# A decoder trunk with three attention mixers: low parts of query stacks and weight chunks made on VectorE in the stage of compressed blocks

## What is computed

```python
kcmp = compress(kc, pe_k, wk1, wk2)
vcmp = compress(vc, pe_v, wv1, wv2)
cend = jnp.arange(ncmp) * CMP_STRIDE + CMP_LEN - 1
dist_c = t[:, None] - cend[None, :]
valid_c = dist_c >= 0
sc = jnp.einsum('bsgrd,bcgd->bgrsc', q, kcmp).astype(jnp.float32) * scale
sc = sc - slopes[:, :, None, None] * dist_c.astype(jnp.float32)
p_cmp = jax.nn.softmax(jnp.where(valid_c, sc, NEG), axis=-1) * valid_c
o_cmp = jnp.einsum('bgrsc,bcgd->bsgrd', p_cmp.astype(vcmp.dtype), vcmp)
imp = jnp.einsum('bgrsc,cj->bsgj', p_cmp, overlap_matrix(ncmp, n_slc))
...
score = jnp.where(causal[:, None, :], jnp.where(forced[:, None, :], FORCE, imp), NEG)
_, idx = lax.top_k(score, topn)
...
return gates[..., 0:1] * o_cmp + gates[..., 1:2] * o_slc + gates[..., 2:3] * o_win
```

## Time and profile before

| | |
|---|---|
| median of three executions | 933.0 us |
| the profiled execution's own time | 934.59 us |
| its span | 932.5 us |
| mean granted TensorE clock | 0.946 |
| TensorE (PE) busy | 835.9 us, 90% |
| VectorE (DVE) busy | 568.5 us, 61% |
| ScalarE (ACT) busy | 432.5 us, 46% |
| GpSimd (POOL) busy | 171.4 us, 18% |

### The profile page before, as it was taken

How to read it: one execution, slowest core, us unless ns; L and a number is a source line. 1 busy time by engine, 2 the same in 40 slices (tenths; PEclk the granted TensorE clock), 3 DMA queues, 4 the chain that set the end, 5 groups by cost and what they waited for, 6 DMA issues and landing times. The chain is left out here.

```text
span 932.5 us, 19153 instructions
## 1 busy us (share of the span) xinstructions
PE 835.9 (90%) x7748; PEld 706.9 (76%) x7748; DVE 568.5 (61%) x1305; ACT 432.5 (46%) x969; POOL 171.4 (18%) x123
## 2 busy tenths in 40 slices
PE   3999999969898888689889993989999999979997
PEld 3899887757686767578778872878887988868885
DVE  4841111136989888567639982878787877843332
ACT  5621111034565555357433322677777787732221
POOL 0233000030312231021045310141010323031220
PEclk9999999989899999699979995999999999979999
DMA  7220226052314122061254316000001111032431
GB/s 267 101 114 1 73 97 169 12 148 82 97 64 123 36 91 69 27 174 44 68 134 107 91 46 174 2 2 2 3 2 47 47 48 47 3 113 94 133 135 45
DMA packets 31942, 73.04 MB, mean 78 GB/s; under 512 B 5104, under 2 KB 13680, under 8 KB 30832
## 3 DMA queue, kind: packets, MB, share of 16 engines
q1 hardware_dynamic: 31856, 71.83, 24.8%
HBM read 55.57 MB, written 16.25 MB: 77 GB/s over the span
## 5 line engine op out<-in xcount | busy, mean ns | idle before, releaser
L1677 DVE SCALAR_TENSOR_TENSOR n_probsT_low<-n_turned,n_probsT_high 128x512 f16<-128x512 f32 (+3 forms) x192 | 94.4, 520 | 32.1 <-ACT n_probsT_high L1612 29.8
L1602 ACT ACTIVATE n_probs<-n_probs,n_negated_max 128x640 f32<-128x640 f32 (+7 forms) x128 | 94.0, 734 | 26.4 <-DVE n_negated_max L1668 25.7
L1612 ACT ACTIVATE n_probsT_high<-n_turned 128x512 f16<-128x512 f32 (+3 forms) x192 | 81.1, 457 | 37.7 <-PE n_turned L657 35.4
L657 PE MATMUL n_turned<-identity,n_probs 128*128 128x128 f32 x528 | 82.2, 280 | 16.1 <-ACT n_probs L1602 15.7
L1770 PE MATMUL n_scores<-w_and_keys_high,stacks 128*128 128x256 f32 (+2 forms) x192 | 78.5, 409 | 3.9 <-DVE n_negated_max L1668 2.5
L657 PEld LDWEIGHTS n_turned<-identity,n_probs 128*128 128x128 f32 x528 | 61.0, 143 | 23.7 <-ACT n_probs L1602 17.9
L153 POOL TENSOR_TENSOR w_and_keys_low<-w_raw,w_and_keys_high 128x1024 fp32r<-128x1024 f32 x15 | 38.2, 2546 | 154.1 <-ACT w_and_keys_high L146 153.9
L1771 PE MATMUL n_scores<-w_and_keys_low,stacks 128*128 128x256 f32 (+2 forms) x192 | 63.2, 336 | 0.0
L1668 DVE CUSTOM_DVE_ANT_0 n_probs<-n_scores,n_bias_full 128x1024 f32<-128x1024 f32 (+3 forms) x64 | 48.3, 754 | 20.0 <-PE n_scores L1774 19.9
L580 PE MATMUL nat<-stacks,xT_high 128*128 128x256 f32 (+1 forms) x192 | 56.0, 292 | 2.8 <-DVE stacks L452 2.6
L785 ACT ACTIVATE a_probsT_high<-a_turned 128x512 f16<-128x512 f32 (+3 forms) x48 | 21.8, 489 | 74.0 <-PE a_turned L657 74.0
(11 more groups left out here) (266 smaller groups left out, 2540.8 us busy)
## 6 DMA issues: line engine op xcount, KB each, us to landing
w_raw<-in_w_feat SPq DMA_DIRECT2D x23, 512.0 KB, 3.7
features<-staged SPq DMA_DIRECT2D x30, 256.0 KB, 2.0
a_raw<-features SPq DMA_DIRECT2D x36, 128.0 KB, 2.7
s_raw<-features SPq DMA_DIRECT2D x18, 256.0 KB, 4.3
branches_b_c<-in_x SPq DMA_DIRECT2D x8, 512.0 KB, 5.1
silu_gates<-staged SPq DMA_DIRECT2D x16, 256.0 KB, 2.0
gatesT<-silu_gates SPq DMA_DIRECT2D x8, 512.0 KB, 5.4
keys_and_w_out_raw<-in_w_out SPq DMA_DIRECT2D x4, 1024.0 KB, 4.8
```

What stands on the lines that cost most here:

```text
L657: mm = nc.tensor.transpose(dst[:, j, :], src[:, c:c + P], ident[:, :])
L1602: nc.scalar.activation(pr[:, n % PS, 0:w], pr[:, n % PS, 0:w], ACT.Exp, scale=-1.0, bias=nmax[:, hb % 4, qt:qt + 1], accum_out=sums[:, hb ...
L1612: nc.scalar.activation(pth[:, g % GS, 0:k, :], tp[g % TS][:, 0:k, :], ACT.Copy, scale=PSCALE).then_inc(t_high, 1)
L1677: nc.vector.scalar_tensor_tensor(out=ptl[:, g % GS, 0:k, :], in0=tp[g % TS][:, 0:k, :], scalar=PSCALE, in1=pth[:, g % GS, 0:k, :], op0=ALU ...
```

## The change

The low parts of stacks and chunks in `cmp_phase` move from GpSimd to VectorE, with the same operands. `Filler` gets `split_low_on_vector`, and VectorE's stream gets its own `stack(j)`. Stacks 0 and 1 and chunk 1 are the first instructions of VectorE in the stage; stack 2 stands ahead of the first `gate_out`. In the pass of head h the low part of stack h+3 follows directly behind the shift (for h = 0 to 4; the key stack 8 comes in the pass of head 6), and a chunk's low part stands ahead of `norm(h)` for h = 0, 2 and 4. GpSimd's block is gone, so that GpSimd has no instruction in this stage.

```diff
--- before.py
+++ after.py
@@ -144,6 +144,14 @@
             act.wait_ge(self.sig.loaded, 16 * (self.loads + j - 1))
             act.wait_ge(self.sig.done, self.before + 2 * (j - 1))
         self.nc.scalar.copy(self.ring.hi[:, (self.first + j) % 2, :, :], self.ring.raw[:, :, :]).then_inc(self.sig.high, 1)
+
+    def split_low_on_vector(self, dve, j):
+        if not self.has(j):
+            return
+        s = (self.first + j) % 2
+        dve.wait_ge(self.sig.high, self.splits + j)
+        self.nc.vector.tensor_tensor(self.ring.lo[:, s, :, :], self.ring.raw[:, :, :],
+                                     self.ring.hi[:, s, :, :].bitcast(F32), ALU.subtract).then_inc(self.sig.low, 1)
 
     def split_low(self, pool, j):
         if not self.has(j):
@@ -1390,19 +1398,37 @@
                                         ALU.is_equal).then_inc(chosen, 1)
                 dve.wait_ge(chosen, g + 1)
 
+            def stack(j):
+                dve.wait_ge(stack_high, j + 1)
+                if j < C_H:
+                    low = qs[HD:P, j, :]
+                    nc.vector.tensor_tensor(low, raw[HD:P, j % 2, :], low.bitcast(F32), ALU.subtract).then_inc(q_ready, 1)
+                else:
+                    nc.vector.tensor_tensor(klw, raw[:, j % 2, :], khw.bitcast(F32), ALU.subtract).then_inc(q_ready, 1)
+
+            stack(0)
+            stack(1)
+            fill.split_low_on_vector(dve, 1)
             dve.wait_ge(gate_exp, 1)
             ch.link(nc.vector.tensor_scalar(gate[:, :, :], gate[:, :, :], 1.0, 2 * PSCALE, ALU.add, ALU.mult))
             ch.link(nc.vector.reciprocal(gate[:, :, :], gate[:, :, :]))
             ch.link(nc.vector.memset(unsel[:, :, :, :], 0.0))
             dve.wait_ge(const_in, 48)
+            stack(2)
             fill.gate_out(dve, 0)
             shift(0)
             fill.gate_out(dve, 1)
             for h in range(C_H):
                 if h + 1 < C_H:
                     shift(h + 1)
+                if h + 3 < C_H + 1 and h != C_H - 3:
+                    stack(h + 3)
+                if h == C_H - 2:
+                    stack(C_H)
                 if h >= 1:
                     c_low_part(h - 1)
+                if split_at(h):
+                    fill.split_low_on_vector(dve, split_at(h))
                 norm(h)
                 if h >= 2:
                     c_write_out(h - 2)
@@ -1415,27 +1441,6 @@
             c_write_out(C_H - 2)
             fill.gate_out(dve, LEAD + C_H - 1)
             c_write_out(C_H - 1)
-
-        @block.gpsimd
-        def _(pool):
-            def stack(j):
-                pool.wait_ge(stack_high, j + 1)
-                if j < C_H:
-                    low = qs[HD:P, j, :]
-                    nc.gpsimd.tensor_tensor(low, raw[HD:P, j % 2, :], low.bitcast(F32), ALU.subtract).then_inc(q_ready, 1)
-                else:
-                    nc.gpsimd.tensor_tensor(klw, raw[:, j % 2, :], khw.bitcast(F32), ALU.subtract).then_inc(q_ready, 1)
-                pool.wait_ge(q_ready, j + 1)
-
-            stack(0)
-            stack(1)
-            fill.split_low(pool, 1)
-            stack(2)
-            for h in range(C_H):
-                if h + 3 < C_H + 1:
-                    stack(h + 3)
-                if split_at(h):
-                    fill.split_low(pool, split_at(h))
 
         @block.tensor
         def _(pe):
```

## The result

The change makes the kernel slower: median 956.71 us (955.45 to 957.44, five executions) against 933.7 us (932.86 to 935.32, five: the three listed ahead and two more) of before, ratio 1.0237 with a 95% interval of 1.022 to 1.0254. The profiled execution took 956.83 us.

What follows compares the result with a forecast made beforehand. In the compressed-block stage TensorE was taken to set the pace, VectorE close behind. Terms 14.2 (passes 2 to 4) + 5.1 (start, passes 0 and 1) + 1.7 + 1.5 (passes 5, 6) = 22.5 us: median 955.5, range 945 to 964.

Steps and rivals of the forecast that it cites:

- Amount: VectorE in the compressed-block stage: 15.6 us of subtractions added, 12.4 us of stalls given back, 3.2 us more work.
- Start, pass 0: Stage start: first stack after 1.2 instead of 2.4 us; then head 0's normalisation done at 493.2, 3.8 us later.
- Pass 1: Until its L193 ends: 506.3 instead of 501.25, +5.1 us with start and pass 0, including 2.3 for TensorE's low clock.
- Passes 2 to 4: VectorE waits 6.4 us for load and cast in each; passes of 13.5, 15.6 and 13.1 us, together +14.2 us.
- Passes 5 to 7 and the end: Pass 5 +1.7 us for a low-clock spell, pass 6 +1.5 us for the key stack, pass 7 and end unchanged.
- Rival 1: Loads on time, passes 2 to 4 wait only for casts: 7.8 us less than forecast, 947.7; chance 0.05.
- Rival 2: Stage gets faster because VectorE loses 12.4 us of stalls: 3.7 us less than before, 929.3; chance 0.04.
- Rival 3: TensorE at the low clock also through passes 5 to 7: 6.6 us more, 962; chance 0.12.

Runs made afterwards that it cites:

- e4: The change with SP's stack loads one store earlier and the low parts behind the normalisation of the pass: 930.6 us, ratio 0.9972 to the kernel before.
- e5: The change with 12 useless matmuls on TensorE ahead of the waits of heads 0, 3 and 4: 953.4 us, ratio 1.0218 to the kernel before.
- e1: The kernel before, subtractions left on GpSimd, but VectorE waits for the casts at the change's places in the passes: 953.7 us, ratio 1.0223.
- e2: The change with SP's load of each stack from the fifth on issued one store earlier: 944.6 us, ratio 1.0137 to the kernel before.
- e3: The change with its low parts behind the normalisation of the pass, SP's order unchanged: 937.5 us, ratio 1.0045 to the kernel before.
- e9: Repeat of e4 (the change, loads earlier and low parts behind the normalisation): 929.9 us, ratio 0.998 to the kernel before.
- e10: Repeat of e8 (the kernel before, all subtractions on GpSimd, SP's loads one store earlier): 934.1 us, ratio 1.0024 to the kernel before.
- e8: The kernel before, all subtractions on GpSimd, with SP's loads one store earlier: 934.5 us, ratio 1.002 to the kernel before.

## Why the prediction was right

The forecast was 955.5 us, within 945 to 964; measured 956.7. For each step, after's times are moved by 0.9 us, since TensorE began the stage at 461.97 and not at 462.88.

- **Amount.** 15.6 us of work for 12.4 us of stalls: L1405 and L153 took 1.22 us each where the earlier trace rows gave 1.23, and the stalls are gone. Net 2.8 us of VectorE's busy time on the page, 3.2 expected. That this in itself costs nothing is shown by e4.
- **Start, pass 0.** TensorE's first scores came 1.9 us earlier in the stage: 1.2 from VectorE's faster subtraction, as forecast, and 0.7 because the first load landed earlier, which nothing in the change explains. The second L201 ended at 482.0, 482.9 on before's clock, forecast 483.1. The weights of head 0 were normalised at 492.5 (L1363 follows at 492.53), 493.4 on before's clock, forecast 493.2.
- **Pass 1.** The low clock that I took behind TensorE's idle time came (0.63 from 493.7 to 498.0) and cost 2.0 us against e5, where I had 2.3. L201 ended at 505.44, or 506.3 on before's clock: +5.1 us, as forecast.
- **Passes 2 to 4.** 13.2, 16.7 and 13.7 us, forecast 13.5, 15.6 and 13.1. Together +15.7 and not +14.2. The term that was sized too small is load and cast: 6.0, 7.3 and 7.0 us from L201's end to the cast's end, where I carried 6.4 over from two loads of before. e1, e2 and e3 show that this chain is the cause, each from another side: kept without the work it costs nearly as much, shortened it costs 9 us less by the ratios, moved off the normalisation's path 18 us less.
- **Passes 5 to 7 and the end.** From the last of these L201 to the next stage 583.44 - 549.10 = 34.3 us against 560.46 - 529.27 = 31.2: +3.1, forecast 1.7 + 1.5. Both parts came: from head 4's transposes to head 5's 11.1 us for 9.3, from head 5's to head 6's 8.6 for 7.3.
- **Rival 1**, casts alone, was priced at 7.8 us less than the forecast by three passes of 34.4 us in all; e2 made just this kernel and its passes sum to 34.4, 9.2 us less than the change's own 43.7. The start with passes 0 and 1 gained another 2.7, which I had left out, and passes 5 to the end lost 2.4 in the profiled execution, where the granted clock was 0.65 for 13.5 us behind head 4's transposes.
- **Rival 2**, the relief. The rule of the Trainium skill (SBUF — State Buffer, "Who interferes with whom") holds in every kernel here that has both engines at work: VectorE's own subtraction took 2.6 us behind GpSimd's and 1.22 without. It did not decide, because the waits were eight to ten times the half microsecond per pass that I had put as the turning point. e9 against e10 gives 4.2 us, near the 3.7 at which I had priced this rival, but from head 1's transposes on the two take the same time, so the agreement doesn't confirm that price.
- **Rival 3**, the low clock through passes 5 to 7, did not come: the granted clock was 0.92 from 550 to 560 us and 1.00 from there to 580.

One detail was wrong though it moved no term: I wrote that TensorE would idle some 4 us in each of passes 0 to 4. Ahead of the transposes it idled 5.3, 1.4, 1.7, 4.1 and 5.0 us. For heads 1 and 2 TensorE came late itself, behind a spell at the low level each time: 0.63 from 493.7 to 498.0, and 0.64 and 0.51 in the two stretches of 2 us from 510 to 514.

## To carry to other kernels

When work moves to another engine, cost its place in that engine's queue before its amount: an engine in order waits for the slowest input of any instruction in it, and here 4 us of waiting per pass came from a 1.2 us subtraction. Follow the wait back through every queue (VectorE, ScalarE's cast, SP's load, the store ahead of it, VectorE again), as the last link may be the engine itself. Then the wait is a loop, and its load and cast (6.0 to 7.3 us a pass here) stay however fast the engine is. The same work behind the instruction that others wait for, with its load issued one step earlier, cost nothing and gave at most 0.2 to 0.3%. And look at every instruction that the moved work pushes back, not only at the first that is waited for: in e3 a wait of 2.21 us for a write-out was followed by 10.3 us at about half the clock.

Stalls of an engine that doesn't set the pace are not time. VectorE stalled for 12.4 us in the stage before, and exchanging the stalls for 15.9 us of subtractions in a harmless place moved the part behind head 1's transposes by 1.2 us at most (60.1 in e4 and 61.6 in e9 for 61.3).

## What I had not expected

With the loads early and GpSimd at work (e8, e10) the kernel is not faster but 0.2% slower, with intervals that begin at 1.0: VectorE stalls for 15.1 us of e8's stage where before had 12.4. The cause of the 0.2% was not tested. And a part of the work can cost nearly as much as all of it: four of the thirteen subtractions, in the wrong place, made 1.76% of the 2.37%.
